# Every second weight column as the stationary tile of the up products, with w_down's rows loaded to match

## The reference, cut to what matters

```
def swiglu(h, w_gu, w_down):                      # block 1, D_FF = 2816
    a, b = jnp.split(h @ w_gu, 2, axis=-1)
    return (jax.nn.silu(a) * b) @ w_down
...
m = jnp.square(jax.nn.relu(h2 @ w_up[l])) @ w_down[l]     # block 2, D_FF_2 = 4096
x = x + _rms_norm(m, g_post_mlp[l])
```

## Time and profile before

| what | us |
|---|---|
| median of 3 runs | 822.99 |
| lowest, highest | 822.92, 823.28 |
| span of the profiled execution | 821.9 |

### The profile page before, as it was taken

How to read it: one execution, slowest core, us unless ns; L and a number is a source line. 1 busy time by engine, 2 the same in 40 slices (tenths; PEclk the granted TensorE clock), 3 DMA queues, 4 the chain that set the end, 5 groups by cost and what they waited for, 6 DMA issues and landing times.

```text
span 821.9 us, 14292 instructions
## 1 busy us (share of the span) xinstructions
PE 797.3 (97%) x5493; PEld 695.4 (85%) x5493; DVE 428.3 (52%) x684; ACT 418.8 (51%) x641; POOL 376.9 (46%) x181
## 2 busy tenths in 40 slices
PE   6999999999899999999999999999999999999996
PEld 4778877887778999999998889999887988899985
DVE  4675568984667533422336747645455333423435
ACT  5335426455846444444444955654756544444443
POOL 3126000000164654666545986565464554666452
PEclk9999999999999999999999999999999999999999
DMA  9984577134953666555654796434455556566551
GB/s 320 302 285 133 161 235 253 54 102 103 345 168 116 198 193 190 175 179 185 192 166 132 227 205 186 130 105 132 150 167 167 157 182 197 180 190 191 184 149 51
DMA packets 94397, 146.61 MB, mean 178 GB/s; under 512 B 15742, under 2 KB 64111, under 8 KB 94353
## 3 DMA queue, kind: packets, MB, share of 16 engines
q1 hardware_dynamic: 92896, 143.23, 55.9%
q0 software_dynamic: 1424, 2.77, 1.3%
q10 hardware_dynamic: 32, 0.01, 0.0%
HBM read 144.93 MB, written 1.06 MB: 178 GB/s over the span
## 4 chain that ended last, share of the span: by engine, by line
PE 85%; DVE 6%; issue 3%; POOL 2%; ACT 2%; DMA 2%; DVEq 0%; SPq 0%; ACTq 0%; POOLq 0%
PE bank L1877 82%; POOL w_lo L628 2%; ACT w_hi L693 1%; PE bank L2147 1%; PE bank L1968 1%; DMA raw<-in_w_mod 1%; DMA x<-in_x 1%; DMA gate_mlp_b<-gate_rows 1%; DVE x L1829 1%; PE bank L2455 1%; DVE w_lo L1196 1%; DVE stat L1513 1%; DVE x L1642 0%; DVE o_lo L1734 0%; DVE bank L1641 0%
## 5 line engine op out<-in xcount | busy, mean ns | idle before, releaser
L628 POOL TENSOR_TENSOR w_lo<-raw,w_hi 128x1024 fp32r<-128x1024 f32 (+2 forms) x150 | 361.8, 2428 | 318.7 <-ACT w_hi L693 318.5
L693 ACT ACTIVATE w_hi<-raw 128x1024 fp32r<-128x1024 f32 (+1 forms) x218 | 226.1, 1045 | 217.3 <-PE bank L1877 192.5
L1196 DVE TENSOR_TENSOR w_lo<-raw,w_hi 128x1024 fp32r<-128x1024 f32 x71 | 87.0, 1236 | 141.3 <-ACT w_hi L693 141.2
L1877 PE MATMUL bank<-z_hi,w_hi 128*128 128x256 f32 x384 | 109.0, 284 | 0.2
L1877 PE MATMUL bank<-z_hi,w_lo 128*128 128x256 f32 x384 | 107.2, 279 | 0.0
L1877 PE MATMUL bank<-z_lo,w_hi 128*128 128x256 f32 x384 | 107.1, 279 | 0.0
L1877 PE MATMUL bank<-n_hi,w_hi 128*128 128x256 f32 x352 | 100.4, 285 | 1.0 <-POOL w_lo L628 1.0
L1877 PE MATMUL bank<-n_hi,w_lo 128*128 128x256 f32 x352 | 99.8, 284 | 0.0
L1877 PE MATMUL bank<-n_lo,w_hi 128*128 128x256 f32 x352 | 99.0, 281 | 0.0
L1877 PE MATMUL bank<-w_hi,mlp_h_hi 128*128 128x512 f32 x216 | 85.3, 395 | 0.0
L1877 PE MATMUL bank<-w_hi,mlp_h_lo 128*128 128x512 f32 x216 | 85.2, 395 | 0.0
(11 more groups left out here) (419 smaller groups left out, 1553.0 us busy)
## 6 DMA issues: line engine op xcount, KB each, us to landing
raw<-in_w_in SPq DMA_DIRECT2D x54, 512.0 KB, 4.5
raw<-in_w_down SPq DMA_DIRECT2D x54, 512.0 KB, 3.7
raw<-in_w_gu SPq DMA_DIRECT2D x44, 512.0 KB, 3.5
raw<-in_w_up SPq DMA_DIRECT2D x32, 512.0 KB, 3.7
raw<-in_w_mod SPq DMA_DIRECT2D x24, 512.0 KB, 4.1
raw<-in_w_mod SPq DMA_DIRECT2D x32, 256.0 KB, 6.1
raw<-in_w_out SPq DMA_DIRECT2D x12, 512.0 KB, 4.0
raw<-in_w_in SPq DMA_DIRECT2D x8, 336.0 KB, 3.0
```

Of the source, the lines that this page charges most:

```text
L628: nc.gpsimd.tensor_tensor(wl[:, w % SPL, 0:size], raw[:, slot_raw, 0:size], wh[:, w % SPL, 0:size].bitcast(F32), ALU.subtract).then_inc(s_ ...
L693: nc.scalar.activation(wh[:, w % SPL, 0:size], raw[:, slot_raw, 0:size], ACT.Copy).then_inc(s_hi, 1)
L1196: V.tensor_tensor(wl[:, w % SPL, :], raw[:, slot_raw, :], wh[:, w % SPL, :].bitcast(F32), ALU.subtract).then_inc(s_lod, 1)
L1877: return nc.tensor.matmul(out_, l, r_, start=start, stop=stop, skip_group_check=True)
```

## The change

The new helper `by_channel_pairs` takes for j = 0 the even columns and for j = 1 the odd columns of a block's 256 as the stationary tile, with a step of two floats (8 bytes) between columns. Hidden channel 256 g + 2 p + j then sits on partition p, and chunk q of w_down is loaded with the rows 256 g + 2 p + q. The number, order and size of instructions are the same on every engine, and so are their waits; only the access pattern of 1056 + 768 stationary tiles and the HBM addresses of 22 + 32 loads differ. A partition still receives one contiguous row of 4 KB in each of these loads; rows for neighbouring partitions now lie 8 KB apart instead of 4 KB.

```diff
-        dn_v = w_down.rearrange("(r p) n -> r p n", p=P)
+        dn_v = w_down.rearrange("(g p two) n -> g two p n", p=P, two=2)
...
-                src = dn_v[bass.ds(4 * i + 2 * g + q, 1)].rearrange("r p n -> p (r n)")
+                src = dn_v[bass.ds(2 * i + g, 1), q].rearrange("r p n -> p (r n)")
...
-        dn2_v = w_down2.rearrange("(r p) n -> r p n", p=P)
+        dn2_v = w_down2.rearrange("(g p two) n -> g two p n", p=P, two=2)
...
-                src = dn2_v[bass.ds(6 * i + 2 * g + q, 1)].rearrange("r p n -> p (r n)")
+                src = dn2_v[bass.ds(3 * i + g, 1), q].rearrange("r p n -> p (r n)")
...
+            def by_channel_pairs(s, k0, xh, xl, outs, made, order):
+
+                for kk in order:
+                    if made:
+                        made(k0 + kk)
+                    for j, (o, first) in enumerate(outs):
+                        c = slice(T * kk + j, T * kk + T, 2)
+                        ins = mm3(o, wh[:, s, c], wl[:, s, c], xh[:, k0 + kk, :], xl[:, k0 + kk, :],
+                                  first and k0 + kk == 0, k0 + kk == KT - 1)
+                return ins
...
-                    by_channel(s, 4, 4 * (q % 2), nh, nl, T,
+                    by_channel_pairs(s, 4 * (q % 2), nh, nl,
...
-                    by_channel(s, 4, 4 * q, zh, zl, T, [(ps[g % 3][:, T * j:T * j + T], j == 0) for j in range(2)],
+                    by_channel_pairs(s, 4 * q, zh, zl, [(ps[g % 3][:, T * j:T * j + T], j == 0) for j in range(2)],
```

## The result

| what | before | changed |
|---|---|---|
| median us | 823.13 | 827.21 |
| lowest, highest us | 822.59, 824.08 | 826.85, 828.49 |
| ratio, 95% interval | | 1.0048 (1.0033 to 1.0063) |
| span of the profiled execution, us | 821.9 | 825.0 |

The changed kernel is slower by 0.48%, about 4 us. Device time lies some 1.8 us above the span in every run that gives both. The profiled execution of before, with 821.9, lay in the upper part of that kernel's spread: a second trace of it has a span of 820.5, and a second trace of the changed kernel has 824.7. These two pairs differ by 3.1 and 4.2 us. The 1.1 us outside the span, given ahead of the prediction, came from setting a median of 822.99 beside an execution that must have taken some 823.7.

The account below looks back on a forecast made before the run. PE bounds the kernel through the matmul pitch in both MLPs. Profiled span 821.9 us, plus 1.1 outside and 0 to 0.2 for the change, gave 823.0; the range of 8 in 10 was 812 to 840.

Parts of the forecast that it names:

- the two PE pieces: Unbroken matmul stretches on PE's chain: 165.57 us of MLP 1 and 178.99 us of MLP 2.
- the prediction's own sign: It would be wrong if the up products' pitch, start to start, moved by 1 ns or more either way.
- likeliest case: No change in the up products' pitch, 120.0 and 117.7 ns; 823.0 us, own range 821.4 to 824.6, chance 0.38.
- the reads that get in each other's way: Rival: stationary and moving reads in the up products disturb each other, 1 to 9 ns a product, 825 to 839.4; chance 0.27.
- n = 2 of the earlier trace: Moving operands of `level`, two floats before the address jumps: 9 ns more a product than n = 4, taken for step two.
- The floor: Pitch a contiguous stationary tile needs when it alone decides, 109 ns; with 9 ns for the step, 118 ns.
- the cover: In the up products the moving stream hides the longer stationary load: 118 ns against 120.0 and 117.7, 0 to +0.2 us.
- The upper ends: Costly bounds for the up products' stationary load: 167 ns, 87.5 us more; at half rate 216 ns, 176.9 us more.
- n = 1: Moving operands of `level`, one float before the address jumps: 58 ns more a product than n = 4.
- The rival built on it, 910.5: Every element of the up products' stationary tile costs its own read, 87.5 us more; 910 and above had chance 0.13.
- The pitch that settles lower: Rival: the up products' pitch falls to 113 ns, gaining up to 11.0 us, 812.0 to 821; chance 0.20.
- w_down's rows: Loads of w_down: 0 to +0.8 us of landing each, hidden by 10 us of slack; late loads had chance 0.02.

Follow-up runs that it names:

- e3: Changed kernel with contiguous stationary tiles again and the up products' moving operand cut to 128 columns in seven of eight products; 812.54 us.
- e4: Changed kernel, step-two stationary tiles kept, with the up products' moving operand cut to 128 columns in seven of eight products; 824.82 us.
- e6: Changed kernel with every fourth column instead of every second in the up products' stationary tiles; 1029.43 us.
- e7: The kernel before, unchanged, run once more for a second trace; span 820.5 us.
- e2: The kernel before with only w_down's rows loaded in the new order, stationary tiles contiguous; ratio 1.0002 (0.9990 to 1.0014).
- e11: The kernel before, stationary tiles contiguous, with a step of two floats in the up products' moving operand; 1015.39 us.

## Why the prediction was right, and where it wasn't

**What bounds the kernel** was read rightly: the two PE pieces, and in them the pitch, took the whole difference. The price list also held, 1 ns of pitch for 1.82 us: 2.3 ns gave 4.2 us. The measured 827.2 lies within 812 to 840, but only because that range took in the rivals on both sides. By the prediction's own sign, a pitch that moves by 1 ns or more, the working of its likeliest case was wrong.

**The likeliest case was not what happened.** The forecast was no change, 823.0, with 0.38; the result is in the case of the reads that get in each other's way, 825 to 839.4, near its lower end. Slower as such had 0.42, the largest of the three.

**The price of the step, 9 ns from n = 2 of the earlier trace rows**, was near: the load's pitch alone rose by 5.6 to 6.6 (e3, e4). The floor it was laid on, 109 ns, was 2.5 to 3 too low (111.5 to 111.9 in e3). The 109 is real in the burst it was read from, but n = 8 to 64 of the earlier trace rows already gave (1.95 - 0.28)/15 = 111 ns for the pair nearest to this one. The two errors cancelled by luck: 118 ns forecast for a load of step two, 117.1 to 118.5 measured.

**The step that failed is the cover.** The prediction let the pitch be the larger of the two streams, 118 against 117.7 and 120.0, and so called the cost 0 to 0.2 us. It measured 4.2 us. With both streams near 117 ns the pair took 120.0 and 121.0, 2.3 ns over the same loops without a step at their lower pitch. When both are about equally long they no longer hide each other wholly; why, no run shows. Part of this was in sight: MLP 1's 120.0 was already above its moving stream's 117.7. It was read as a property of MLP 1's addresses; e7 shows it as one of two values that the same kernel takes. And n = 2 of the earlier trace rows, read from start to start, stood at 120 ns and not at the 118 of the sum.

**The upper ends were badly priced.** The price of 58 ns from n = 1 gave 167 ns for a load with each float in its own 16 bytes; e6 has 232. In the n = 1 row two tiles are read in turn, so the 128 floats come out of 64 pieces, two times each. It was not the one-float-a-piece case it was taken for, and its 166 ns stay unexplained. The pause in these bursts, put between their halves, lies behind the first product (253, 223 and 213 ns to the second), which changes the prices by some 3 ns at most. The rival built on it, 910.5, would have needed such a tile, which a step of two isn't.

**The pitch that settles lower**, 113 ns as in the earlier trace rows, came in no trace of an MLP at full length. Its price doesn't stand against e4 either: a load of step two alone needs 117.

**w_down's rows** were right in size and cover: 4.1 us of landing in the changed kernel and 4.3 in e2, where 3.7 to 4.5 was stated, and e2 shows them hidden.

**The rule of the Trainium skill** ("Advanced Engine Details and Errata", section SBUF Cachelines), two hits on a line, would have given 823.0. It was set against n = 2 of the earlier trace rows, and the row was the better guide, in sign and in the load's own price. The central forecast followed neither fully: the cover brought it back to 823.0.

## What to carry to other kernels

Where PE's pitch is set by how fast operands are read, count the 16-byte pieces that each operand passes, not its elements. Here, for steps up to four floats and at 1.8 ns a piece, a moving fp32 operand of 256 columns (64 pieces) hides a contiguous stationary tile (32 pieces, 112 ns) and no longer quite one of step two (64 pieces). Before a stream is called hidden, ask whether it is clearly shorter than the one that hides it; two about equal streams here cost 1 to 3 ns more than either. And where one trace differs from its median by more than the forecast effect, take the pitch of a loop from two traces.

## What the runs showed of the hardware

The pitch of these products follows 1.8 ns for each 16 bytes of a partition that the longer operand stream passes: 232.2 ns for a stationary tile of 128 floats at step four, 172.8 at step three, 117.1 to 118.5 at step two with a short moving operand, 233.1 for a moving operand of 256 floats at step two, 232.5 for one of 512 without a step. A contiguous stationary tile is the exception, with 111.5 to 111.9 ns where its 32 pieces would make 58, and a moving operand read from two tiles in turn, float by float, is another, with 166 ns. Steps of more than four floats weren't run. The load's shown duration rises too, 188, 198, 261 and 330 ns for steps of one to four, but it also depends on what runs beside it (192 and 208 ns for contiguous tiles in e3 and e11). One and the same loop stood at 118.7 ns in one trace and at 120.0 in another, and held it over all its trips; with the other kernels the values 117.3 and 121.0 were seen as well. What decides it stays open, and so does why the two streams together cost 1 to 3 ns more than the longer alone: that they meet in SBUF is an argument, no run here shows it.
